# Experts' weights in DRAM as blocks of 512 columns, loaded in pieces of 2 KB

## The reference

```python
def swiglu(x, w_gate, w_up, w_down):
    return (jax.nn.silu(x @ w_gate) * (x @ w_up)) @ w_down
# per token: sigmoid scores, the best 4 of 8 groups, the best 6 experts, gates normalised x 2.5
routed = routed_experts(x, eidx, gates, w1, w3, w2)    # w1, w3: (64, 1024, 256), w2: (64, 256, 1024)
shared = swiglu(x, ws1, ws3, ws2)
return routed + shared
```

## Time and profile before

| | |
|---|---|
| median of 3 runs | 2932.34 us (2920.26 to 2938.7) |
| the profiled execution's own time | 2939.54 us |
| its span | 2937.9 us |
| TensorE (PE) busy | 2574.6 us, 88% |
| VectorE (DVE) / ScalarE (ACT) / GpSimd (POOL) busy | 57% / 34% / 47% |
| mean granted TensorE clock | 0.943 |
| moved by DMA | 641.40 MB, mean 218 GB/s |
| loads of experts' weights | 65 of 2 MB and 65 of 1 MB |

### The profile page before, as it was taken

How to read it: one execution, slowest core, us unless ns; L and a number is a source line. 1 busy time by engine, 2 the same in 40 slices (tenths; PEclk the granted TensorE clock), 3 DMA queues, 4 the chain that set the end, 5 groups by cost and what they waited for, 6 DMA issues and landing times. The chain is left out here.

```text
span 2937.9 us, 50941 instructions
## 1 busy us (share of the span) xinstructions
PE 2574.6 (88%) x11953; PEld 2059.9 (70%) x11954; DVE 1683.2 (57%) x2642; ACT 1008.8 (34%) x1599; POOL 1379.8 (47%) x1127
## 2 busy tenths in 40 slices
PE   7999999999678888499889889979988899989891
PEld 4787777767567777387668668767766688767671
DVE  4663655573156666655755565656487544675543
ACT  3222433234122221213433344434355422453422
POOL 1210045420236666421755565655567644566554
PEclk9999999999889999699999999999999999999995
DMA  6865868565654443357886787877689866788657
GB/s 266 309 243 197 291 231 306 190 233 184 230 190 165 167 169 129 151 123 198 281 243 155 232 265 207 260 240 191 180 285 325 265 167 158 192 290 261 188 112 264
DMA packets 160487, 641.40 MB, mean 218 GB/s; under 512 B 28764, under 2 KB 42400, under 8 KB 128288
## 3 DMA queue, kind: packets, MB, share of 16 engines
q1 hardware_dynamic: 101424, 459.70, 42.6%
q0 software_dynamic: 58992, 180.78, 25.9%
HBM read 463.08 MB, written 177.33 MB: 218 GB/s over the span
## 5 line engine op out<-in xcount | busy, mean ns | idle before, releaser
L2120 DVE TENSOR_TENSOR w_exp_lo<-w_exp,w_exp_hi (+1 forms) x256 | 385.3, 1546 | 89.7 <-ACT w_exp_hi L2058 79.7
L1973 POOL TENSOR_TENSOR w_exp_lo<-w_exp,w_exp_hi (+1 forms) x130 | 327.0, 2538 | 17.2 <-ACT w_exp_hi L2063 13.5
L2246 PE MATMUL ps_h<-w_exp_hi,x_exp_t_hi 128*128 (+1 forms) x1216 | 312.6, 399 | 23.0 <-ACT w_exp_hi L2058 17.2
L2058 ACT ACTIVATE w_exp_hi<-w_exp (+1 forms) x256 | 257.3, 1053 | 215.6 <-issue 122.0
L2246 PE MATMUL ps_h<-w_exp_lo,x_exp_t_hi 128*128 (+1 forms) x1216 | 311.3, 398 | 17.0 <-DVE w_exp_lo L2120 17.0
L2246 PE MATMUL ps_h<-w_exp_hi,x_exp_t_lo 128*128 (+1 forms) x1216 | 322.1, 407 | 0.0
L2033 POOL DMA_INDIRECT sum_d<-w_shared_raw,give x136 | 251.0, 1846 | 90.3 <-DVE w_shared_raw L2158 44.5
L2246 PEld LDWEIGHTS ps_h<-w_exp_hi,x_exp_t_hi 128*128 128x128 f32 x1216 | 229.6, 190 | 81.9 <-ACT w_exp_hi L2058 17.4
L2246 PEld LDWEIGHTS ps_h<-w_exp_lo,x_exp_t_hi 128*128 128x128 f32 x1216 | 228.2, 188 | 76.7 <-issue 21.8
L1134 PE MATMUL ps_p<-wa_hi,hx_split 128*128 128x512 f32 x1088 | 277.1, 400 | 4.9 <-DVE kvqg_out L100 4.0
L2158 DVE SCALAR_TENSOR_TENSOR w_shared_raw<-ps_y,give,g_row 128x512 f32<-128x512 f32 x272 | 191.3, 745 | 128.6 <-PE ps_y L2246 86.3
(11 more groups left out here) (269 smaller groups left out, 4371.8 us busy)
## 6 DMA issues: line engine op xcount, KB each, us to landing
w_exp<-in_experts SPq DMA_DIRECT2D x64, 2048.0 KB, 11.2
w_exp<-in_experts SPq DMA_DIRECT2D x65, 1024.0 KB
hx_split<-hx_d SPq DMA_DIRECT2D x54, 1024.0 KB, 5.6
rec_m<-rec_d SPq DMA_DIRECT2D x16, 1536.0 KB, 8.7
hx_d<-hx_split SPq DMA_DIRECT2D x18, 1024.0 KB, 5.3
wm_rest<-in_w_mod_rest POOLq DMA_DIRECT2D x16, 1024.0 KB, 6.0
rec_d<-kvqg_out SPq DMA_DIRECT2D x48, 256.0 KB, 4.3
xt<-in_xt POOLq DMA_DIRECT2D x18, 512.0 KB, 8.9
```

The costliest lines, as they stand in the source:

```text
L1973: pool.tensor_tensor(w[1][:, piece(e, i)].bitcast(F32R), raw(e, i), w[0][:, piece(e, i)], ALU.subtract).then_inc(wd_lo, 1)
L2058: act.activation(w[0][:, piece(e, i)].bitcast(F32R), raw(e, i), ACT.Copy).then_inc(gu_hi, 1)
L2120: dve.tensor_tensor(w[1][:, piece(e, i)].bitcast(F32R), raw(e, i), w[0][:, piece(e, i)], ALU.subtract).then_inc(gu_lo, 1)
L2246: last = pe.matmul(out, x[:, j * P:(j + 1) * P].bitcast(F32R), w_part[:, bass.ds(w_at + j * stride, 512)].bitcast(F32R), start=(start and ...
```

## The change

The host lays each expert's 128 x 6144 weights out as 12 blocks of 128 x 512, one behind the other. The kernel reads the same columns into the same places, 8 blocks for gate/up and 4 for down. In DRAM a block's row is 2 KB long, so that each transfer is made of pieces of 2 KB, the next of the same partition 256 KB further on. Issue order, waits and destinations stay as they are. The transfers that load expert 2 after the shared blocks, written out before, now call `load`.

```diff
-            sp.dma_start(pre[:].rearrange("p a n -> p (a n)"), io["experts"][0, :, 0:4 * D]).then_inc(pre_loaded, 16)
+            sp.dma_start(pre[:].rearrange("p a (c n) -> p (a c) n", n=512),
+                         io["experts"][0, 0:8].rearrange("c p n -> p c n")).then_inc(pre_loaded, 16)
...
-    out["experts"] = np.concatenate(both)
+    out["experts"] = np.ascontiguousarray(np.concatenate(both).reshape(65, P, 12, 512).transpose(0, 2, 1, 3))
...
             def load(e, slot, first, size, done):
-                src = io["experts"][bass.ds(e, 1)].rearrange("a p n -> (a p) n")
+                src = io["experts"][bass.ds(e, 1), first // 512:(first + size) // 512].rearrange("a c p n -> (a p) c n")
                 to = slot * W + first
-                sp.dma_start(w_raw[:, to:to + size], src[:, first:first + size]).then_inc(done[slot], 16)
+                sp.dma_start(w_raw[:, to:to + size].rearrange("p (c n) -> p c n", n=512), src).then_inc(done[slot], 16)
...
-            sp.dma_start(w_raw[:, 0:WE], io["experts"][2, :, 0:WE]).then_inc(gu_loaded[0], 16)
+            load(2, 0, 0, WE, gu_loaded)
             sp.wait_ge(wd_lo, N_D)
-            sp.dma_start(w_raw[:, WE:W], io["experts"][2, :, WE:W]).then_inc(wd_loaded[0], 16)
+            load(2, 0, WE, WD, wd_loaded)
```

## The result

| | before | after |
|---|---|---|
| median of the runs | 2935.5 us (4 runs) | 2889.7 us (4 runs) |
| ratio | | 0.9849, 95% interval 0.9801 to 0.9896 |
| profiled execution, span | 2937.9 us | 2884.5 us |

A forecast was written before the change was run, and what follows sets the result against it. TensorE was taken to set the pace in the expert stage, with DMA not far behind. From the profiled 2939.5 us, - 80 (waits 60, slow clocks 20) + 25 gave 2884.5 us, 2877 for the median; range 2830 to 2945.

The forecast's parts named there:

- waits for gathered blocks: TensorE's 34 waits in the expert stage, 89.3 us; two thirds of them were to go, 60 us.
- slow clock behind them: TensorE's transposes run slow after long gather waits; 10 of 14 cases at 2.0 us each saved, 20 us.
- waits for weights: TensorE's waits for `h_exp_t_lo` and `w_exp_lo`; loads 1.7 us later, 0.85 us in each of 30 blocks, +25 us.
- The turn: On the DMA engines queues alternate piece by piece; a POOL piece waits 0.087 in place of 0.640 us, 4.4 us per 8.
- how much sooner a transfer lands: Scatters and gathers beside an expert load were to land 2 to 4 us sooner, quiet ones unchanged.
- rival A: Engines read 71 KB of load ahead of a POOL transfer whatever the piece size; half the gain, 2917 us; chance 0.20.
- rival B: A DMA turn holds several pieces, so no gain: 2944 us, past 3100 us at sixteen pieces; chance 0.10.
- The price per kB: Expert loads in 2 KB pieces cost more engine time: +0.4 us an expert taken, at most +0.9 us.
- The landing of a gate/up load: Expert load ends later as the gather's pieces pass ahead: 1.3 us plus 0.4 us, 1.7 us late.
- C: Expert loads' reads at a 256 KB pitch cost more, making DMA the bound beyond 106 ns a piece; 3020 us; chance 0.08.

The follow-up runs named there:

- short_down: Against the kernel before: 2 KB pieces as in the kernel after, but from expert 2 on only 512 of down's 2048 columns are loaded; ratio 0.9846.
- fine_ring_2k: Against the kernel before: 2 KB pieces, gate/up load cut into four of 1024 columns, each issued and split as soon as possible; ratio 0.9889.
- rows_padded: Against the kernel before: old order of the experts' array with 256 unused bytes after each chunk, so 2 KB pieces lie 2.25 KB apart; ratio 0.9875.

## Why the prediction was right

**The sum.** It went from 2939.5 us to 2884.5 and, for the median, 2877; measured were 2886.1 us for the profiled execution and 2889.7 as a median of runs against 2935.5: 0.985 where 0.981 was forecast.

| term | forecast | measured in the traces |
|---|---|---|
| waits for gathered blocks | -60 | -65.5 (89.3 to 23.8) |
| slow clock behind them | -20 | -10.9 (the same 6317 matmuls in 1359.9 for 1370.8 us) |
| waits for weights | +25 | +17.9 (44.9 to 62.8) |
| sum | -55 | -58.5; the routed blocks take 56.4 us less, the span is 53.4 us shorter |

The two ends of the last line differ because the routed blocks also begin 2.9 us later. The medians, 2935.5 and 2889.7, are 46 us apart: the traced execution of before (2939.5) lies 4 us above its median and that of after (2886.1) 4 us below. The forecast, which started from a traced execution, has that in its favour.

**The term that was mis-sized: the slow clock.** I took 10 of 14 waits at 2.0 us each, the size found behind the longest wait. Of the 16 long waits of before 11 have transposes of more than 1.4 us behind them and five have 1.09 to 1.37, against 1.04 undisturbed, so a long wait does not always bring a slow clock. With 14 long waits fewer, 10.9 us is an estimated 0.8 us for each, not 2.0. Of the 10.9 us the transposes alone give 9.4 (153.5 to 144.1 us).

**The turn.** That a turn is one piece was the step that carried the forecast, and it holds in both traces: 86 to 82 packets before, 79 to 79 after. The row of experiments bears out its direction, not its law: at 8 KB the turn's price is halved and the time unmoved. The waits there are 23 us fewer (64.5 + 46.9 against 89.3 + 44.9), but the median is only 2 us lower (2920.7 against 2923.1). Most of that gap lies in the trace of before: it took 2939.5 us and that of 8 KB 2923.6, 16 us less, so trace against trace the time follows the waits. That execution of before probably waited longer than most; no second trace of it shows by how much.

**What failed in the mechanism: how much sooner a transfer lands.** I expected 2 to 4 us beside a load. In the stretch with an expert per block (2152 to 2250 us) the gathers and then the scatters of after land in:

```profile
DMA to landing us min/median/max: 9.1/9.5/9.9
...
DMA to landing us min/median/max: 9.5/9.6/9.8
```

Before, it was 8.6 and 10.1: the median did not fall for gathers and fell by 0.5 us for scatters; only the spread and the longest (12.0 and 12.3 us) went clearly down. Over all routed blocks the longest landing of a gather went from 14.1 to 11.0 us and the median from 6.4 to 6.6. By my own signs this speaks against me twice: the 70 KB ahead of a scatter are rival A's sign, unchanged median landings rival B's. B is ruled out by the turns (below). A described one half rightly: 3.6 us of load still go ahead of a scatter. Its price (2917 us, a ratio of 0.995) is outside the measured interval. That the waits were made by the longest landings, the half that changed, fits both traces but was not tested by itself. That the waits fell by 65 us, close to the 60 of the forecast, though the typical landing did not come sooner, is in part luck.

**The loads.** The price per kB went up by 3.6 ns, 0.7 us an expert, where I took 0.4 and bounded it at 0.9. The landing of a gate/up load went up by 3.3 us, not 1.7; that GpSimd's queue has 81% of the engines while both move would do this, but it was not taken apart. The +25 us were costed in the stretches with an expert per block, and there the waits for weights did not rise. TensorE's from 2152 to 2250 us, before and then after:

```profile
PE ps_y L2246 <- DVE h_exp_t_lo L2135: 10.0, 7, 2.3
PE ps_h L2246 <- DVE w_exp_lo L2120: 6.1, 4, 2.6
...
PE ps_y L2247 <- DVE h_exp_t_lo L2136: 12.9, 6, 2.9
PE ps_h L2247 <- DVE w_exp_lo L2121: 1.5, 3, 0.7
```

So 16.1 us became 14.4, and the 18 us more came elsewhere. They hang on loads (40 of the 48.9 us, as shown above), but a quarter fewer bytes does not shorten them (`short_down`), nor does an earlier first piece for ScalarE (`fine_ring_2k`). The chain I costed them by (load, split, next load, in those 30 blocks) is therefore not shown; the term came out near only in its size.

**The rivals.** The times given for A and B count from the median (2932.3 us), that for C from the profiled execution (2939.5), which moves them by 7 us against each other and changes no verdict. B (several pieces to a turn) is excluded by 79 to 79. With it, the rule of the Trainium skill (DMA: Bandwidth & Descriptors, "Queues, rings and completion order") that an engine drains a packet of typically 9 to 17 descriptors before it switches does not describe these two queues: in both traces one piece was one turn. C (dear reads at a 256 KB pitch): the pieces cost 46.7 ns per kB, 96 ns each, below the 106 ns from which DMA would set the pace on average; and `rows_padded`, with reads 2.25 KB apart, is not told from after.

## What to carry to other kernels

Where a large prefetch and small urgent transfers share the DMA engines, look at how both move together: here a turn was one piece of each queue, so that the prefetch's piece size set the urgent one's share, and 2 KB was enough. It moves waiting from one stream to the other, so count both kinds of waits before and after, and look at the longest landings as well as the median ones. Before reordering transfers on a queue, find the loop of landing and issue that runs through it: 2 us put into one that had 1 us to spare cost 7.5% here (1.0755 against 1 with the large pieces, 1.0584 against 0.9849 with the small ones). And read a wait by what the waited-for engine was standing at: `h_exp_t_lo` hid a load in one kernel and a list in another.

## What the runs showed of the hardware

A scatter issued beside a load saw 69 packets of 16 KB or 541 of 2 KB over the 16 engines go first, some 70 KB per engine and 3.4 to 3.6 us both times; without a load its pieces moved within 1 us of its issue. After that the two queues took turns of one piece each, 86 to 82 and 79 to 79, so that their shares went by the sizes of the pieces: 34% of the engines' time for GpSimd's queue beside 16 KB pieces, 81% beside 2 KB ones. Pieces cost 43.1, 43.3, 44.6, 46.7 and 50.0 ns per kB at 16 (down 8), 8, 4, 2 and 1 KB as the loads of this kernel ran, beside the other queue.
